# Block differences of `w_down` made by VectorE during the input projections, `w_o` loaded in parts, and norms whose first pass waits for the statistics alone

## What is computed

```
h = layer_norm(x)
z = h @ w_in                      # 2224 columns: GLA q, k, v, g, a_lr and MLA c_q, c_kv, k_r
GLA:  chunks of 64, state s, o = q exp(b) s + causal(q k) v, then rms_norm and silu(g)
MLA:  prompt attention (8 heads, causal, 1040 keys); sample attention over 4096 cached latents
h1 = layer_norm(alpha*h + concat(og, om) @ w_o)
a, up = split(h1 @ w_ffn_in);  conv = causal depthwise conv of width 3 over a
y = layer_norm(alpha*h1 + (silu(conv) * up) @ w_down)      # w_down: 2816 x 1024
```

## Time and profile before

| | |
|---|---|
| median of three runs | 1601.74 us (1594.39 to 1605.3) |
| the profiled execution | 1591.53 us, its span 1590.0 us |
| mean granted clock of PE | 0.975 |
| busy: PE, PEld, DVE, ACT, POOL | 94%, 79%, 61%, 41%, 20% |
| bytes moved by DMA | 217.65 MB |

### The profile page before, as it was taken

How to read it: one execution, slowest core, us unless ns; L and a number is a source line. 1 busy time by engine, 2 the same in 40 slices (tenths; PEclk the granted TensorE clock), 3 DMA queues, 4 the chain that set the end, 5 groups by cost and what they waited for, 6 DMA issues and landing times.

```text
span 1590.0 us, 29074 instructions
## 1 busy us (share of the span) xinstructions
PE 1498.0 (94%) x11025; PEld 1261.3 (79%) x11025; DVE 968.9 (61%) x1733; ACT 655.9 (41%) x1232; POOL 319.1 (20%) x413
## 2 busy tenths in 40 slices
PE   5999999889899979999999999999999999999994
PEld 5989997656566655555788999999999998678883
DVE  6615302655465545556668877877788784456686
ACT  2256322543355543234222555545545452434430
POOL 2101000210342533432011002222222222100002
PEclk9999999989799989999999999999999999999997
DMA  7221111201353554666224133334334436969552
GB/s 246 90 68 58 54 38 31 71 21 38 132 186 106 178 222 156 214 215 212 93 87 122 37 108 123 116 127 133 127 125 133 133 120 223 348 222 294 180 186 106
DMA packets 140167, 217.65 MB, mean 137 GB/s; under 512 B 11578, under 2 KB 91064, under 8 KB 138632
## 3 DMA queue, kind: packets, MB, share of 16 engines
q1 hardware_dynamic: 121530, 143.96, 28.3%
q0 software_dynamic: 18400, 72.36, 13.0%
q10 hardware_dynamic: 144, 0.07, 0.0%
HBM read 165.66 MB, written 50.69 MB: 136 GB/s over the span
## 4 chain that ended last, share of the span: by engine, by line
PE 63%; DVE 6%; DMA 2%; issue 2%; ACT 1%; POOL 1%; another core or an unknown queue 0%; SPq 0%; ACTq 0%; DVEq 0%; POOLq 0%
PE ps L2308 9%; PE ps L2307 9%; PE ps L2306 9%; PE ps L1648 5%; PE ps L1268 4%; PE ps L2905 3%; PE ps L1669 3%; PE ps L2907 3%; PE ps L2906 3%; PE ps L1305 2%; PE ps L210 2%; PE ps L212 2%; PE ps L211 2%; PE ps L1695 2%; PE ps L1282 2%
## 5 line engine op out<-in xcount | busy, mean ns | idle before, releaser
L2306 PE MATMUL ps<-t_hi,op_hi 128*128 128x266 f32 (+1 forms) x672 | 192.2, 286 | 2.4 <-DVE gap_hi L2530 2.4
L2308 PE MATMUL ps<-t_hi,op_lo 128*128 128x266 f32 (+1 forms) x672 | 192.9, 287 | 0.0
L2307 PE MATMUL ps<-t_lo,op_hi 128*128 128x266 f32 (+1 forms) x672 | 192.7, 287 | 0.0
L210 PE MATMUL ps<-w_hi,hT_hi 128*128 128x256 f32 (+2 forms) x504 | 142.2, 282 | 3.4 <-DVE hT_lo L324 3.4
L2308 PE MATMUL ps<-h1T_hi,op_lo 128*128 128x266 f32 x504 | 144.1, 286 | 0.0
L2307 PE MATMUL ps<-h1T_lo,op_hi 128*128 128x266 f32 x504 | 143.4, 285 | 0.0
L2306 PE MATMUL ps<-h1T_hi,op_hi 128*128 128x266 f32 x504 | 143.4, 284 | 0.0
L212 PE MATMUL ps<-w_hi,hT_lo 128*128 128x256 f32 (+2 forms) x504 | 141.5, 281 | 0.0
L211 PE MATMUL ps<-w_lo,hT_hi 128*128 128x256 f32 (+2 forms) x504 | 141.4, 280 | 0.0
L2732 DVE TENSOR_TENSOR ring_lo<-d_raw,ring_hi 128x1024 fp32r<-128x1024 f32 x77 | 94.8, 1237 | 59.5 <-ACT ring_hi L2728 59.0
L2728 ACT ACTIVATE ring_hi<-d_raw 128x1024 fp32r<-128x1024 f32 x77 | 81.7, 1060 | 118.4 <-DMA d_raw<-t_res 61.7
(11 more groups left out here) (364 smaller groups left out, 3500.4 us busy)
## 6 DMA issues: line engine op xcount, KB each, us to landing
f_raw<-in_w_ffn_in SPq DMA_DIRECT2D x88, 256.0 KB, 3.5
g_res<-gap_lo SPq DMA_DIRECT2D x22, 528.0 KB, 3.6
t_mix<-in_w_down SPq DMA_DIRECT2D x44, 256.0 KB
t_res<-t_mix SPq DMA_DIRECT2D x22, 512.0 KB, 3.9
g_mix<-g_res POOLq DMA_DIRECT2D x11, 1024.0 KB, 5.3
s_res<-g_mix POOLq DMA_DIRECT2D x11, 1024.0 KB, 4.2
d_raw<-in_w_down SPq DMA_DIRECT2D x22, 512.0 KB, 7.0
d_raw<-s_res SPq DMA_DIRECT2D x44, 256.0 KB, 3.6
```

The costliest lines, as they stand in the source:

```text
L210: nc.tensor.matmul(out, ah, bh, start=start, stop=False)
L2306: nc.tensor.matmul(o, ah, bh, start=FIRST_IN[q] and k == 0, stop=False, skip_group_check=again)
L2307: nc.tensor.matmul(o, ah, bl, start=False, stop=False, skip_group_check=again)
L2308: last = nc.tensor.matmul(o, al, bh, start=False, stop=k == 3, skip_group_check=again)
```

## The change

**Differences.** `mix_w` now runs on DVE, with the same four subtractions and waits, and in the projections. Two units stand between the two `cumulate` calls, two after slab 5, five after slab 6 (units 4 to 8), six after slab 7 (9 to 14), seven after slab 8 (15 to 21). The loads and stores move from SP's queue to POOL's, in the same order as before, and begin when the latents are normed (`rms_done`). `t_mix` lies at another address, in space that is free from then until the preparation of MLA; so `act_prep` and `dve_prep` wait for the last stores.

**Loads.** Half of `w_o` comes in four parts of 512 KB, one after every second set from step 4 on, and `w_uv` behind them. The gathers of set 2 wait until the first two steps of sample scores are done.

**Norms.** `norm_apply` is cut in two: `norm_center` waits for `stats_done` alone, `norm_scale` for `rstd_done`. In the last stage each tile's norm follows its own statistics at once, and the last tile is scaled and stored in two halves.

The semaphores of another table (`g_mix`) now share those of the differences, which changes no order.

```diff
-        def norm_apply(j, n, x, g=lng, b=lnb):
+        def norm_center(j, n, x, g=lng):
 
             dve_settle(nc.vector.scalar_tensor_tensor(out=x, in0=x, scalar=stat[0:n, 16 * j + 12:16 * j + 13],
                                                       in1=g[0:n, :], op0=ALU.subtract, op1=ALU.mult))
+
+        def norm_scale(j, n, x, b=lnb):
+
             return nc.vector.scalar_tensor_tensor(out=x, in0=x, scalar=stat[0:n, 16 * j + 14:16 * j + 15],
                                                   in1=b[0:n, :], op0=ALU.mult, op1=ALU.add)
+
+        t_mix = [at(f"t_mix{i}", [P, 4, 256], o) for i, o in enumerate((6464, 10560))]
+        t_res = nc.dram_tensor("t_res", (FC // 2, P, 4, 512), F32, kind="Internal").ap()
+        mix_loaded = [sem(f"mix_loaded{i}") for i in range(2)]
+        mix_stored = [sem(f"mix_stored{i}") for i in range(2)]
+        mix_step = sem("mix_step")
+        T_STORED = 16 * (FC // 2)
+
+        def load_mix(pool, n):
+            j, e = divmod(n, 2)
+            for o in range(2):
+                k = P * (2 * j + o)
+                src = ins["w_down"][k:k + P, :].rearrange("p (c n) -> p c n", c=2)[:, :, 256 * e:256 * e + 256]
+                pool.dma_start(t_mix[e][:, 2 * o:2 * o + 2, :], src).then_inc(mix_loaded[e], 16)
+
+        def store_mix(pool, n):
+            j, e = divmod(n, 2)
+            pool.wait_ge(mix_step, n + 1)
+            pool.dma_start(t_res[j, :, :, 256 * e:256 * e + 256], t_mix[e][:, :, :]).then_inc(mix_stored[e], 16)
+
+        def mix_w(dve, n):
+
+            j, e = divmod(n, 2)
+            b11, b12, b21, b22 = [t_mix[e][:, i, :] for i in range(4)]
+            dve.wait_ge(mix_loaded[e], 32 * (j + 1))
+            dve_settle(nc.vector.tensor_tensor(b11, b12, b11, ALU.subtract))
+            dve_settle(nc.vector.tensor_tensor(b12, b22, b12, ALU.subtract))
+            dve_settle(nc.vector.tensor_tensor(b22, b22, b11, ALU.subtract))
+            nc.vector.tensor_tensor(b21, b21, b22, ALU.subtract).then_inc(mix_step, 1)
...
                     dve.wait_ge(gain_loaded, 32)
+                dve.wait_ge(stats_done, j + 1)
+                norm_center(j, n, xs[j % XS][0:n, :])
                 dve.wait_ge(rstd_done, j + 1)
-                norm_apply(j, n, xs[j % XS][0:n, :]).then_inc(h_ready, 1)
+                norm_scale(j, n, xs[j % XS][0:n, :]).then_inc(h_ready, 1)
...
-            for m in range(2):
-                cumulate(dve, m)
+            cumulate(dve, 0)
+            for n in range(2):
+                mix_w(dve, n)
+            cumulate(dve, 1)
             offsets(dve)
             w_lo_dve(dve, 5)
+            for n in range(2, 4):
+                mix_w(dve, n)
             products(dve)
-            for s in (6, 7, 8):
+            for s, a, b in ((6, 4, 9), (7, 9, 15), (8, 15, FC)):
                 w_lo_dve(dve, s)
+                for n in range(a, b):
+                    mix_w(dve, n)
...
             pool.wait_ge(rms_done, NT)
+            load_mix(pool, 0)
+            load_mix(pool, 1)
...
+            store_mix(pool, 0)
+            for n in range(1, FC):
+                if n < FC - 1:
+                    pool.wait_ge(mix_stored[(n - 1) % 2], 16 * ((n - 1) // 2 + 1))
+                    load_mix(pool, n + 1)
+                store_mix(pool, n)
...
         def act_prep(act):
+            for e in range(2):
+                act.wait_ge(mix_stored[e], T_STORED)
...
             dve.wait_ge(mla_loaded, 48)
+            for e in range(2):
+                dve.wait_ge(mix_stored[e], T_STORED)
...
-        def load_wo(h):
-
-            nc.sync.dma_start(wo_raw[:, 4 * h:4 * h + 4, :], ins["w_o"][512 * h:512 * h + 512, :]
-                              .rearrange("(k p) n -> p k n", p=P)).then_inc(wo_loaded[h], 16)
...
-        def move_w(sp):
-            sp.wait_ge(prep_act, act_at[index[prep[-1]] + 1])
-            sp.wait_ge(prep_dve, dve_at[index[prep[-1]] + 1])
-            load_mix(sp, 0)
-            load_mix(sp, 1)
-            for n in range(FC):
-                j, e = divmod(n, 2)
-                if 1 <= n < FC - 1:
-                    sp.wait_ge(mix_stored[1 - e], 16 * ((n - 1) // 2 + 1))
-                    load_mix(sp, n + 1)
-                sp.wait_ge(mix_step, n + 1)
-                sp.dma_start(t_res[j, :, :, 256 * e:256 * e + 256], t_mix[e][:, :, :]).then_inc(mix_stored[e], 16)
-
-        def mix_w(pool, n):
-
-            j, e = divmod(n, 2)
-            b11, b12, b21, b22 = [t_mix[e][:, i, :] for i in range(4)]
-            pool.wait_ge(mix_loaded[e], 32 * (j + 1))
-            pool_settle(nc.gpsimd.tensor_tensor(b11, b12, b11, sub))
-            pool_settle(nc.gpsimd.tensor_tensor(b12, b22, b12, sub))
-            pool_settle(nc.gpsimd.tensor_tensor(b22, b22, b11, sub))
-            nc.gpsimd.tensor_tensor(b21, b21, b22, sub).then_inc(mix_step, 1)
...
+        def load_wo(k, n):
+
+            nc.sync.dma_start(wo_raw[:, k:k + n, :], ins["w_o"][P * k:P * k + P * n, :]
+                              .rearrange("(k p) n -> p k n", p=P)).then_inc(wo_loaded[k // 4], 16)
 
         def sp_e(sp):
             sp.wait_ge(prep_done, index[("qn", 3, 2)] + 1)
             sp.dma_start(wide[:, :], ins["c_wide"]).then_inc(mla_loaded, 16)
-            move_w(sp)
-            sp.wait_ge(score_done, N_ATT)
-            load_wo(1)
+            for k in range(4):
+                sp.wait_ge(ss_done, step_of(2 * k + 2))
+                load_wo(4 + k, 1)
             sp.wait_ge(pt_done, pt_base[-1])
             sp.dma_start(w_uv[:, :, :], ins["w_uv"].rearrange("(k p) n -> p k n", p=P)).then_inc(mla_loaded, 16)
 
@@ -1598,14 +1613,12 @@
             load_latents(0)
             out_of_psum(pool, prep[-1])
             load_rotary(0)
-            for n in range(11):
-                mix_w(pool, n)
             pool.wait_ge(score_done, N_ATT // 2)
             load_rotary(1)
-            for n in range(11, 22):
-                mix_w(pool, n)
             for z in range(1, SETS):
                 slot_free(pool, z)
+                if z == 2:
+                    pool.wait_ge(ss_done, 2)
                 load_latents(z)
...
-            act.wait_ge(wo_loaded[h], 16)
+            act.wait_ge(wo_loaded[h], 64 if h else 16)
...
             def tile_norm(i):
                 r = frows(i)
+                dve.wait_ge(stats_done, NT + i + 1)
+                norm_center(i, r, hr[i % 2][0:r, :])
                 dve.wait_ge(rstd_done, NT + i + 1)
-                norm_apply(i, r, hr[i % 2][0:r, :]).then_inc(h1_ready, 1)
+                norm_scale(i, r, hr[i % 2][0:r, :]).then_inc(h1_ready, 1)
...
-            for t in range(NT - 1):
+            for t in range(NT - 2):
                 sp.wait_ge(y_ready, t + 2)
                 sp.dma_start(outs["y_prompt"][0, P * t:P * t + P, :], y[t][:, :]).then_inc(old_loaded, 16)
+            t = NT - 2
+            for h in range(2):
+                c = slice(512 * h, 512 * h + 512)
+                sp.wait_ge(y_ready, NT + h)
+                sp.dma_start(outs["y_prompt"][0, P * t:P * t + P, c], y[t][:, c]).then_inc(old_loaded, 16)
...
+            def center(n, r, x):
+                dve.wait_ge(stats_done, 2 * NT + n + 1)
+                norm_center(n, r, x, ln2g)
+
+            def scale(n, r, x):
                 dve.wait_ge(rstd_done, 2 * NT + n + 1)
-                norm_apply(n, r, x, ln2g, ln2b).then_inc(y_ready, 1)
+                norm_scale(n, r, x, ln2b).then_inc(y_ready, 1)
+
+            def scale_half(n, x, h):
+                c = slice(512 * h, 512 * h + 512)
+                dve.wait_ge(rstd_done, 2 * NT + n + 1)
+                nc.vector.scalar_tensor_tensor(out=x[:, c], in0=x[:, c], scalar=stat[:, 16 * n + 14:16 * n + 15],
+                                               in1=ln2b[:, c], op0=mult, op1=add).then_inc(y_ready, 1)
...
-                if t in (1, 2, 3):
-                    norm(t, P, y[t - 1][:, :])
-                if t >= 3:
-                    norm(t + 1, P, y[t][:, :])
+                center(t + 1, P, y[t][:, :])
+                if t < NT - 2:
+                    scale(t + 1, P, y[t][:, :])
+                else:
+                    scale_half(t + 1, y[t], 0)
+                    scale_half(t + 1, y[t], 1)
```

More of the change, by code:

```diff
@@ L1750, in act_e @@
             act.wait_ge(latent_stored, 96)
-            for e in range(2):
-                act.wait_ge(mix_stored[e], T_STORED)
             def copy(dst, src):
@@ L1957, in sp_f @@
             sp.wait_ge(ss_done, N_S - 1)
-            load_wo(0)
+            load_wo(0, 4)
             sp.wait_ge(ss_done, N_S)
@@ L2573, in build @@
         g_mix = at("g_mix", [P, 4, 512], 5440)
-        g_mix_loaded = sem("g_mix_loaded")
-        g_mix_stored = sem("g_mix_stored")
         s_res = nc.dram_tensor("s_res", (FC // 2, P, 4, 512), F32, kind="Internal").ap()
@@ L2580, in load_g @@
             pool.dma_start(g_mix[:, :, :].rearrange("p (k h) t -> p k (h t)", h=2),
```

(27 more changed lines are left out.)

12 lines of the change are left out of this document (removed).

## The result

The changed kernel took 1616.89 us (median of six runs, 1612.45 to 1618.63), the kernel before 1600.43 (six runs beside it, 1594.39 to 1605.3). The ratio is 1.0095, with a 95% interval of 1.0076 to 1.0114: **16 us or 1% slower**, at the upper edge of the range and far from the 1604.5 of the forecast. The profiled executions lie further apart (1591.53 and 1615.83, spans 1590.0 and 1613.9). Part of that gap isn't the change, as the experiments show. The forecast's range of 1591 to 1617 holds the 1616.89 by 0.1 us; with six runs between 1612.45 and 1618.63 that is chance.

A forecast was written before the change was run, and what follows sets the result against it. PE, busy 1498.0 of 1590.0 us, bounds the kernel. DVE's lateness with clock 8.4, last norm with halves 1.6, pause -6.3, other norms -0.9: +2.8 us, forecast 1604.5 against the 1601.74 median; eight in ten from 1591 to 1617.

The forecast's parts named there:

- rival C: Projections: two tiles refilled no faster than before, 6.0 us a unit; DVE 17.9 late, +15.3 in all, 1617.0 us; chance 0.10.
- The period of a unit, 5.3: Projections, units from 6 on: two loads and the store behind them set a 5.3 us spacing, between 4.8 and 6.0.
- DVE's own cost, 1.8 us a unit: Projections: four subtractions with their waits take DVE 1.8 us a unit, 40 us for 22 units.
- DVE late by 6.4: Start of GLA: DVE is free at 267.3 instead of 260.9, and PE is late by as much.
- The 2 us for the slabs: Projections: transfers for slabs 7 and 8 and the GLA state delay the chain by 2 us, 0 to 3.
- The 2 us for the clock: Behind PE's longer pause at GLA: work at the lower clock level adds 2 us, 0 to 3.
- Slab 8 in time by 3 us: Projections: slab 8 is split at 232.5, PE needs it at 235.5, so 3 us to spare.
- Differences removed from attention, 0: Prompt attention: PE waits for neither POOL nor SP there, so taking the differences away counts as zero.
- The pause, -6.3: Between the attentions: moved loads let ACT's copy follow PE at once, 4.6 us, plus 1.7 of clock; between 0 and -7.5.
- Last norm, +1.9 and tiles 4.93 apart: Norm at the end: POOL is held up while DVE centres; eight tiles take 39.4 us against 37.5, +1.9.
- Rival D: Norm at the end: POOL isn't held up, eight tiles gain 3.9 us, 4.2 with the halves; 1598.7 us; chance 0.08.
- The other norms, -0.9: One norm place in the projections, two at the end of `w_o`: 0.3 us gained at each, between 0 and -1.5.

The follow-up runs named there:

- the late norm: The kernel before, with every tile's norm in the last stage put behind the next tile's sum and statistics; ratio 0.999 (0.9979 to 1.0002).

## Why the prediction was right or wrong

**Direction: right; mechanism: right where most of the time goes, the chain of transfers that makes DVE late for GLA; size: wrong.** The forecast was +2.8 us, measured are +15 to +16.5. What happened is rival C, to which I gave 0.10: the two tiles aren't refilled faster than before. That its 1617.0 meets the 1616.89 is luck. It had 17.9 us for DVE and 3 for the clock, where DVE came 20.65 late and the clock took nothing, and its -5.6 for the rest is made of other terms than the -6.4 of the marks above.

- **The period of a unit, 5.3, measured 6.29.** This is the step that failed: fifteen rounds, 15 us. The mis-sized term is the store's landing. I took the 4.09 from its issue to the next loads as the upper end; on POOL's queue it is 4.1 to 6.2, 4.9 on average. I also read the 6.02 of the earlier trace rows as POOL's slow arithmetic, which DVE would take away. In the ten rounds behind the 6.02 the store is issued on average only 0.4 us after its loads, so that POOL's arithmetic was 0.4 of it at most, and the run with one subtraction shows that DVE's isn't in the round at all. The bound of 6.0 was too low as well.
- **DVE's own cost, 1.8 us a unit: right.** The four subtractions of a unit start 0.46 us apart, 476 ns were expected. It lay where it was hidden.
- **DVE late by 6.4, measured 20.65** (21.2 on the third chip). The 2 us for the slabs were too few, but not by much: the two rounds beside the loads of slab 8 (issued at 211.8) and of the GLA state (236.8) are 7.6 us long, the others 5.5 to 6.9. The 2 us for the clock weren't paid: from 288 us on ACT's operations are 19.7 late.
- **Slab 8 in time by 3 us: wrong**, it was split at 238.54, and PE fell 5.9 us behind, 4.2 standing and the rest at a clock of 0.95 over the 35 us. With the slab in time GLA started no earlier, so this adds nothing; a stop ahead of a larger wait for the same engine is a part of it.
- **Differences removed from attention, 0: measured -5** on the third chip (21.2 to 16.2), and -6 between the first two traces (19.7 to 13.6). On the second it was next to nothing against the run with the loads alone (GLA 19.8 late, the end of attention 19.7), and -1.9 against that with the norms alone (18.9 and 17.0). On the third chip the clock accounts for an estimated 3.4 of the five, 24 us times the difference of 0.14. At the beginning of attention it was 0.58 before and 0.72 after, over nearly the same work:

```profile
404.00:428.00 24.00, 20.40 (x97) 12.22 (x97) 7.92 (x22) 7.15 (x16) 9.55 (x12) 0.58 0.43 144
```

```profile
424.00:448.00 24.00, 19.80 (x108) 11.51 (x108) 9.59 (x28) 8.16 (x18) 3.79 (x4) 0.72 0.16 44
```

  That the missing transfers raise the clock isn't shown, and the second chip speaks against it: over the same windows it was 0.79 with the transfers (norms alone) and 0.72 without (differences alone).
- **The pause, -6.3: the 4.6 came, the rest didn't.** The pause went from 5.51 to 0.86. But the marks above are 13.1 late at its end and 16.1 after the sets, so 3.0 of the 3.1 us gained on that chip were lost again, nearly all of it within 13 us of the product. The clock falls with or without the pause, for about 10 us in either trace; before, 4 of them fell on the pause, and now they fall on work, which by its level and length is an estimated 1.6 of the 3.0. The other 1.4 is a wait of PE for DVE, 0.72 before and 2.09 now:

```profile
595.89 0.63 PE L1695 MATMUL ps<-zt,spt 32*32 32x256 f32 x8 [0.72 <-DVE oacc L1875]
```

```profile
610.21 0.63 PE L1708 MATMUL ps<-zt,spt 32*32 32x256 f32 x8 [2.09 <-DVE oacc L1886]
```

  It is 1.50 in the first trace of the changed kernel and 0.72 in both runs with the loads alone, so it isn't the loads by themselves; its cause is open. Part of my reading was too much: full DMA engines don't make ACT wait by themselves, as the second chip shows. On the chips with the pause it goes away with the loads; what ACT waits for stays unnamed.
- **Last norm, +1.9 and tiles 4.93 apart: measured +2.8 and 5.02.** The scaling began 2.38 us behind the start of the aggregation instead of 2.28. The halves gave 0.5 instead of 0.3. The rule of the Trainium skill in "SBUF — State Buffer", "Who interferes with whom", held in all eight tiles, 1.30 to 1.31 us instead of 0.22. Rival D, without it, was 6.7 us off here, -3.9 against +2.8.
- **The other norms, -0.9: not seen.** On the second chip everything behind the first norms was 2.1 us earlier with the change than without; but it was 1.7 earlier in the run whose norms are those of before. On the third chip the changed kernel is 0.35 us earlier there. Of a real gain no more than 0.4 is left.
- **The rest, about -3.6** between the sample attention and the last norm on the third chip, I had at 0. No experiment was made on it; the run with slab 8 split early, which has the first part alone, gained about 1 there.

What would have shown it: the forecast named a spacing of 6.0 for L337, a clock below 0.9 between the attentions and a wait for slab 8 as its own refutations. The profile has a spacing of 6.29, a clock of 0.86 from 592 to 597 us, and the wait.

## What to carry to other kernels

Where two buffers go round through load, work and store, price the round by its transfers: the loads' issue, the store's issue, and the landing of a store that stands behind other loads on its queue. In that order faster arithmetic doesn't shorten it; what did was to issue the stores from another engine's queue, 5.2 us a unit instead of 6.2. Give such a chain only as many rounds as end before its engine is needed, and leave the others where they were. And before a gain or loss far from the edit is explained, take both kernels' traces on one chip.

## What the runs showed of the hardware

- Chips, or executions on them, differ within the same program by more than the change: the kernel before took 1569.07 us on the second and 1600.32 on the third. With its loads the sets are 9.65 us long on the one and 10.2 to 13.3 on the other, and the pause is 0.86 or 3.96.
- PE stood for 2.34 to 2.41 us in the projections in all fourteen traces, behind the same work. In five the granted clock stayed at 1.00 (2.4 GHz), in nine it fell to 0.50 (1.2 GHz) around the end of the pause or up to 2.2 us behind it, for 3 to 7 us. Where the pause lay in the execution doesn't tell them apart: it ended at 116.43 in the run with slab 8 split early and at 116.41 in that with the late norm, and from 114 to 124 us the clock was 1.00 in the first and 0.66 in the second.

```profile
114.00:124.00 10.00, 7.66 (x40) 6.34 (x40) 4.41 (x13) 4.00 (x13) 3.67 (x3) 1.00 0.00 0
```

```profile
114.00:124.00 10.00, 7.66 (x26) 6.61 (x26) 4.41 (x13) 3.07 (x11) 3.68 (x3) 0.66 0.00 0
```

  It moves all that follows by up to 3.1 us. In the first trace of the changed kernel ACT's outputs are 1.84 us early up to 116 and 1.22 late from 122 on. Neither is the change's: the two traces of the kernel before differ in the same way, the third chip's being 1.5 early up to there and 0.1 late behind it.
- 22 times two loads of 256 KB and a store of 512 KB beside the projections took the DMA share from 0.12 to 0.59 and did PE no harm of their own: from 136 to 213 us, with the transfers beside them, ACT's outputs stay 1.2 us late, but for one at 168 us that is 0.6 later and made up for by the next.
